# Latent attention in a fused two-block kernel: scores of two head pairs at once in four PSUM banks, the rotated parts of four heads on quarters of the array rows

## The reference

```python
def mla_mixer(xn, w_in, q_norm, w_uq, kv_norm, w_ukv, w_o, cos_r, sin_r):
    c = xn @ w_in                                   # 1024 -> 384 + 256 + 32
    cq  = rms_norm(c[..., :384], q_norm)
    ckv = rms_norm(c[..., 384:640], kv_norm)
    kr  = c[..., 640:]                              # one rotated key of 32, shared by all heads
    qf = (cq @ w_uq).reshape(B, S, 16, 64 + 32)
    q_rope = apply_rope(qf[..., 64:], cos_r, sin_r)
    kv = (ckv @ w_ukv).reshape(B, S, 16, 64 + 64)
    k_rope = broadcast(apply_rope(kr, cos_r, sin_r))
    q = concat([qf[..., :64], q_rope]); k = concat([kv[..., :64], k_rope]); v = kv[..., 64:]
    o = causal_attention(q, k, v, scale=96 ** -0.5) # 16 heads, softmax over keys <= query
    return o.reshape(B, S, 1024) @ w_o
```

## Time and profile before

| | |
|---|---|
| median of 3 runs | 1077.17 us (1076.83 to 1077.51) |
| the profiled execution's own time | 1076.59 us |
| span from its first to its last instruction | 1074.8 us |
| PE busy | 1069.1 us (99%) |
| PE weight loads busy | 935.4 us (87%) |
| DVE busy | 839.1 us (78%) |
| ACT busy | 655.6 us (61%) |
| DMA | 191.67 MB, 178 GB/s on average |

### The profile page before, as it was taken

The page is one execution under the profiler, slowest core; times in us unless marked ns, Lnnn a source line. Parts: engine busy times, 40 slices in busy tenths (PEclk is TensorE's granted clock), DMA queues, the critical chain, the costliest instruction groups (busy, mean ns, idle before and its releaser), DMA issues.

```text
span 1074.8 us, 16290 instructions
## 1 busy us (share of the span) xinstructions
PE 1069.1 (99%) x6536; PEld 935.4 (87%) x6536; DVE 839.1 (78%) x1364; ACT 655.6 (61%) x923; POOL 1.3 (0%) x8
## 2 busy tenths in 40 slices
PE   9999999999999999999999999999999999999998
PEld 7778888888898888888889888888977788888888
DVE  7985799886667689988767999776658768997852
ACT  7666567664467765766456577554456765776540
POOL 0000000000000000000000000000000000000000
PEclk9999999999999999999999999999999999999999
DMA  8543446556426064655552366555555434665540
GB/s 318 202 171 119 151 166 234 194 186 215 164 88 245 2 225 163 232 200 187 213 191 109 127 227 235 186 216 186 179 184 181 144 123 150 234 216 193 205 144 30
DMA packets 32091, 191.67 MB, mean 178 GB/s; under 512 B 4496, under 2 KB 6160, under 8 KB 12176
## 3 DMA queue, kind: packets, MB, share of 16 engines
q1 hardware_dynamic: 32016, 190.63, 49.8%
HBM read 189.56 MB, written 1.05 MB: 177 GB/s over the span
## 4 chain that ended last, share of the span: by engine, by line
PE 97%; DVE 1%; ACT 1%; DMA 0%; SPq 0%; issue 0%; DVEq 0%
PE banks L452 21%; PE SB L452 11%; PE TB L452 11%; PE banks L454 11%; PE TB L454 6%; PE SB L454 6%; PE banks L667 4%; PE banks L674 4%; PE banks L668 4%; PE banks L411 4%; PE banks L413 3%; PE banks L412 3%; PE banks L621 2%; PE TB L596 2%; PE SB L583 1%; PE SB L1000 1%
## 5 line engine op out<-in xcount | busy, mean ns | idle before, releaser
L1658 DVE TENSOR_TENSOR wlo<-raw,whi 128x2048 fp32r<-128x2048 f32 (+2 forms) x180 | 396.1, 2202 | 75.1 <-ACT whi L1134 75.0
L1134 ACT ACTIVATE whi<-raw 128x2048 fp32r<-128x2048 f32 (+2 forms) x180 | 330.5, 1840 | 83.8 <-PE TB L454 25.6
L452 PE MATMUL banks<-xx,whi 128*128 128x512 f32 x752 | 262.0, 390 | 0.0
L454 PE MATMUL banks<-xx,wlo 128*128 128x256 f32 x752 | 212.1, 282 | 0.0
L452 PEld LDWEIGHTS banks<-xx,whi 128*128 128x128 f32 x752 | 141.2, 188 | 29.5
L454 PEld LDWEIGHTS banks<-xx,wlo 128*128 128x128 f32 x752 | 142.1, 189 | 0.0
L452 PE MATMUL TB<-xx,whi 128*128 128x512 f32 x336 | 117.8, 390 | 0.3 <-DVE xx L1663 0.3
L452 PE MATMUL SB<-xx,whi 128*128 128x512 f32 x320 | 111.8, 390 | 0.0
L454 PE MATMUL TB<-xx,wlo 128*128 128x256 f32 x336 | 94.7, 282 | 0.0
L452 PE MATMUL banks<-hx,whi 128*128 128x512 f32 x264 | 91.7, 390 | 0.0
L454 PE MATMUL SB<-xx,wlo 128*128 128x256 f32 x320 | 90.2, 282 | 0.0
(11 more groups left out here) (239 smaller groups left out, 1946.0 us busy)
## 6 DMA issues: line engine op xcount, KB each, us to landing
raw<-in_gate SPq DMA_DIRECT2D x44, 1024.0 KB, 4.8
raw<-in_up SPq DMA_DIRECT2D x44, 1024.0 KB, 4.8
raw<-in_down SPq DMA_DIRECT2D x32, 1024.0 KB, 4.8
raw<-in_down SPq DMA_DIRECT2D x16, 768.0 KB, 4.1
raw<-in_d_kq SPq DMA_DIRECT2D x8, 1024.0 KB, 5.0
raw<-in_a_kq SPq DMA_DIRECT2D x6, 1024.0 KB, 5.3
raw<-in_a_o SPq DMA_DIRECT2D x4, 1024.0 KB, 4.9
raw<-in_b_o SPq DMA_DIRECT2D x4, 1024.0 KB, 5.4
```

Source lines behind the costliest of these rows:

```text
L452: e.matmul(po[:, 0:512], wh[:, k, sl], a[:, kk, :, :].rearrange("p w s -> p (w s)"), start=start, stop=stop, skip_group_check=True)
L454: return e.matmul(po[:, 0:256], wl[:, k, sl], a[:, kk, 0, :], start=False, stop=stop, skip_group_check=True)
L1134: e.activation(whi[n % RING][:, 0:nk * w], raw[n % RAW][:, 0:nk * w], ACT.Copy).then_inc(s_hi, 1)
L1658: e.tensor_tensor(wlo[n % RING][:, 0:nk * w], raw[n % RAW][:, 0:nk * w], whi[n % RING][:, 0:nk * w].bitcast(F32), ALU.subtract).then_inc(s ...
```

## The change

It touches stage B alone.

1. Scores are computed for two pairs (a group, g = 0 to 3) at once, into four banks: `SB` for the even pair and `banks0` for the odd one. `pair_scores(j)` becomes `group_scores(g)`.
2. The rotated part of the four heads of a group is computed on four quarters (32) of the array rows, one head and one bank each. `krt` holds the key once and needs no zeros; ACT copies it in one activation in place of two.
3. The banks are dealt out anew: `values` has one bank (3) in place of two, so `values(j)` waits for `output_lo(j-1)` and not for `output_lo(j-2)`; `queries(2)`, `queries(3)` and `value_block(1, 1)` share bank 2; the projection goes to bank 2 (c = 0) and, once the last scores are out, bank 0 (c = 1).
4. The order of the stage is written anew on PE, ACT and DVE. The number of instructions of each kind stays as it was, except for the one activation.

```diff
-        krt = sb("krt", [128, 2, S], F32, mla)
+        krt = sb("krt", [128, S], F32, mla)
...
+        def score_banks(s, j):
+
+            return two_banks[FLIP[s]] if s == B and j % 2 else SB
+
+        def out_bank(s, c):
+
+            return bk(s, (2, 0)[c]) if s == B else bk(s, c)
...
             if s == B:
-                return bk(s, 2 + j % 2)
+                return bk(s, 3)
...
-                        e.wait_ge(s_ol, n_pair(s, j - 2))
+                    else:
+                        e.wait_ge(s_ol, n_pair(s, j - 1))
...
+                def group_scores(g):
+
+
+                    if g == 0:
                         e.wait_ge(s_krt, 1)
-                    if j % 2 == 0:
-                        e.wait_ge(s_qne, j // 2 + 1)
-                        e.wait_ge(s_kne, j // 2 + 1)
-                    if j % 4 == 0:
-                        e.wait_ge(s_qre, j // 4 + 1)
-                    if j >= 1:
-                        e.wait_ge(s_msk, n_pair(s, j - 1))
...
+                    else:
+                        e.wait_ge(s_msk, n_pair(s, 2 * g - 1))
+                    e.wait_ge(s_qne, g + 1)
+                    e.wait_ge(s_kne, g + 1)
+                    e.wait_ge(s_qre, g // 2 + 1)
+                    blocks = ((0, 128, 128), (128, 256, 256))
+                    for j in (2 * g, 2 * g + 1):
+                        for q0, q1, k1 in blocks:
+                            for a in range(2):
+                                p = slice(64 * a, 64 * a + 64)
+                                e.matmul(score_banks(s, j)[:, a, q0:q0 + k1], qn[p, j, q0:q1], kn[p, j, 0:k1],
+                                         start=(q0 == 0), stop=False, skip_group_check=True)
+                    for q0, q1, k1 in blocks:
+                        for t in range(4):
+                            p = slice(32 * t, 32 * t + 32)
+                            last = e.matmul(score_banks(s, t % 2)[:, t // 2, q0:q0 + k1], qr[p, g, q0:q1], krt[p, 0:k1],
+                                            start=False, stop=True, skip_group_check=True)
+                    last.then_inc(s_sc, 2)
...
-                pair_scores(0)
+                group_scores(0)
+                queries(2)
+                group_scores(1)
+                transposes(s, 0)
                 value_block(1, 1)
-                pair_scores(1)
-                queries(2)
-                pair_scores(2)
+                values(s, 0)
+                transposes(s, 1)
                 queries(3)
-                for j in range(8):
-                    transposes(s, j)
-                    if j < 5:
-                        pair_scores(j + 3)
-                    if j >= 5:
-                        project_01(s, u + 10, [j - 2])
-                    values(s, j)
-                    if 1 < j < 5:
-                        project_01(s, u + 10, [j - 2])
-                project_01(s, u + 10, [6, 7])
+                values(s, 1)
+                transposes(s, 2)
+                group_scores(2)
+                values(s, 2)
+                transposes(s, 3)
+                rows(0, 0, 1)
+                values(s, 3)
+                rows(0, 2)
+                transposes(s, 4)
+                group_scores(3)
+                values(s, 4)
+                transposes(s, 5)
+                rows(0, 3, 4)
+                values(s, 5)
+                rows(1, 0, 1, 2)
+                transposes(s, 6)
+                rows(0, 5)
+                values(s, 6)
+                rows(1, 3)
+                transposes(s, 7)
+                rows(1, 4)
+                rows(0, 6)
+                values(s, 7)
+                rows(1, 5, 6)
+                rows(0, 7)
+                rows(1, 7)
```

(`rows(c, ks)` is the output projection into one of the two banks alone, for the pairs `ks`.) The order on DVE, written out after `normalize(1)`:

```diff
+                pair(3)
+                normalize(s, 2)
+                output_lo(s, 0)
+                normalize(s, 3)
+                output_lo(s, 1)
+                lo(u + 12)
+                pair(4)
+                output_lo(s, 2)
+                pair(5)
+                normalize(s, 4)
+                output_lo(s, 3)
+                normalize(s, 5)
+                pair(6)
...
+                output_lo(s, 7)
+                lo(u + 13)
+                lo(u + 14)
```

More of the change, by code:

```diff
@@ L947, in value_block @@
                     else:
-                        e.wait_ge(s_qne, h + 1)
+                        e.wait_ge(s_qne, 1 + 2 * h)
                     for k in range(2):
-                        last = three(bk(s, 2 + h)[:, :], ox[:, 6 + k, 0, sl], ox[:, 6 + k, 1, sl], wh[:, k, :],
+                        last = three(bk(s, 2 + (h if c == 0 else 0))[:, :], ox[:, 6 + k, 0, sl], ox[:, 6 + k, 1, sl], wh[:, k, :],
                                      wl[:, k, :], k == 0, k == 1)
@@ L970, in queries @@
                         weights_here(n)
[L971 to L975, removed]
+                    e.wait_ge(s_ve, b + 1)
+                    last = channels(n, bk(s, (2, 3, 2, 2)[b]), (b % 2) * 256, 3, 3, b)
                     last.then_inc(s_used if b % 2 else s_qn, 1)
@@ new lines, in group_scores, with rows @@
+                    for q0, q1, k1 in blocks:
[4 more added lines that the diff above has]
+                    last.then_inc(s_sc, 2)
+                def rows(c, *ks):
+                    for k in ks:
+                        if k == 0:
+                            weights_here(u + 10 + c)
+                            e.wait_ge(*((s_qne, 4) if c == 0 else (s_msk, n_pair(s, 7))))
+                        e.wait_ge(s_ol, n_pair(s, k))
+                        last = across(u + 10 + c, out_bank(s, c), k, ox, k, k == 0, k == KD - 1)
+                        if k == KD - 1:
+                            last.then_inc(s_used, 1)
@@ L1480, in key_rope @@
                     e.wait_ge(s_lt, 3)
-                    for m in range(2):
-                        last = e.activation(krt[:, m, :], LT[2], ACT.Copy, scale=evenodd[:, m:m + 1])
-                    last.then_inc(s_krt, 1)
+                    e.activation(krt[:, :], LT[2], ACT.Copy).then_inc(s_krt, 1)
                 def keys(b):
@@ L1497, in value_block @@
                         e.wait_ge(s_vp, c + 1)
-                    e.activation(vv[:, h, c * 512:(c + 1) * 512], bk(s, 2 + h)[:, :],
+                    e.activation(vv[:, h, c * 512:(c + 1) * 512], bk(s, 2 + (h if c == 0 else 0))[:, :],
                                  ACT.Copy).then_inc(s_ve, 1)
@@ L1549, in latent_mixer @@
                 exponentials(s, 1)
-                queries(3)
-                for j in range(8):
-                    weights_turned(s, j)
-                    if j < 6:
-                        exponentials(s, j + 2)
-                    if j in (6, 7):
-                        hi(u + 7 + j)
-                    output_hi(s, j)
+                weights_turned(s, 0)
+                value_block(1, 1)
+                exponentials(s, 2)
+                output_hi(s, 0)
+                weights_turned(s, 1)
+                queries(3)
+                exponentials(s, 3)
+                output_hi(s, 1)
+                weights_turned(s, 2)
+                output_hi(s, 2)
+                weights_turned(s, 3)
+                exponentials(s, 4)
+                output_hi(s, 3)
+                weights_turned(s, 4)
+                exponentials(s, 5)
+                output_hi(s, 4)
+                weights_turned(s, 5)
+                exponentials(s, 6)
+                output_hi(s, 5)
+                exponentials(s, 7)
+                weights_turned(s, 6)
+                output_hi(s, 6)
+                weights_turned(s, 7)
+                hi(u + 13)
+                output_hi(s, 7)
+                hi(u + 14)
                 mixer_end(s, u + 10)
@@ L2157, in latent_mixer @@
                 normalize(s, 1)
-                for j in range(8):
-                    if j < 5:
-                        pair(j + 3)
-                    output_lo(s, j)
-                    if j < 6:
-                        normalize(s, j + 2)
-                    if j >= 5:
-                        lo(u + 7 + j)
+                pair(3)
[11 more added lines that the diff above has]
+                pair(6)
+                output_lo(s, 4)
+                pair(7)
+                normalize(s, 6)
+                output_lo(s, 5)
+                normalize(s, 7)
+                output_lo(s, 6)
+                output_lo(s, 7)
+                lo(u + 13)
+                lo(u + 14)
                 mixer_end(s, u + 10)
```

38 lines of the change are left out of this document (9 added, 29 removed).

## The result

The changed kernel takes 1079.83 us (median of 9 runs, 1079.28 to 1080.3), the kernel before beside it 1077.00 (9 runs, 1076.63 to 1077.51). The ratio is 1.0026, 95% interval [1.0017, 1.0035]: slower, where I had forecast 1077.7 and no change, and 0.4 us above my range.

A forecast was written before the change was run, and what follows sets the result against it. PE was taken to bound the kernel, with 97% of the span. New waits of 3.3 less 2.8 of PE's work saved gave +0.5 us, so a median of 1077.7 us; range 1074.2 to 1079.4.

The forecast's parts named there:

- PE's work: Stage B on PE: rotated parts on quarters save 2.56 us, fewer changes of array shape another 0.2; together 2.8 us less.
- change of shape: On PE, switching the shape in which the array is used costs 0.2 us; 27 such switches before, 26 after.
- a group's rotated part: On PE in stage B, four heads on four quarters start together and cost about 0.84 us per group.
- Six waits: In stage B the new orders make PE stand still six times for DVE or ACT, together 3.3 us.
- waits 4 and 5: `transposes(4)` waits for `normalize(4)`, 1.1 us; `transposes(5)` waits for `normalize(5)`, 0.9 us.
- 2 and 3: `values(1)` waits for `output_lo(0)` and `values(3)` for `output_lo(2)`, 0.4 us each.
- 6: `values(6)` waits for `weights_turned(6)`, 0.3 us.
- Behind the stage: After stage B, DVE reaches the residual 2.2 us later, but `lo(u+17)` still lands in time for F1, 0.3 to spare.
- the rival of a delay carried on: After stage B, DVE's extra lateness makes F1 wait for `lo(u+17)` and so on: above 1079.4 us; chance 0.05.
- quarters one after another: In stage B's scores, products run one at a time, 2.8 us per group: about 1083.5 us; chance 0.06.
- Quarters bring no more than halves: In stage B's scores, four 32-row products run two by two, 1.3 + 0.2 per group: net +1.7, 1078.9 us; chance 0.09.
- The waits stay away: In stage B, DVE and ACT come round sooner, leaving only PE's saving: 1074.4 us; chance 0.16.

The follow-up runs named there:

- experiment 1: Changed kernel with one unused 32-byte tile per partition behind the constants, putting tiles such as `hx` and `ox` back at their old addresses: 1077.59 us, ratio 1.0005.
- experiment 7: Changed kernel with 32 unused bytes behind `con` (old addresses) and stage B's orders on PE, ACT and DVE redrawn: 1074.16 us, ratio 0.9975 against the kernel before.
- experiment 4: Changed kernel with rotated parts on halves again, `evenodd` and the key's second copy back (so old addresses): 1078.36 us, ratio 1.0014 against the kernel before.
- experiment 11: Kernel before with 32 unused bytes ahead of `xx` and 96 behind it: 1086.85 us, ratio 1.0091.

## Why the prediction was wrong, by its own steps

**The step that failed** is the sum's silent one: all terms lie in stage B, and of what was removed elsewhere the prediction says only "the one `krt` activation in place of two is off the path". The removed columns `evenodd` were not costed. They carry no time themselves, but without them every tile behind `con` starts 32 bytes earlier, and that costs 2.1 us (experiment 1: 1079.83 - 1077.59 = 2.24, less 0.17 by which before differed between the two sets). In the profile of the changed kernel it is 0.8 ahead of the stage, 0.13 in it (45.62 against 45.49) and 1.03 behind it. No rival had this mechanism; I had not asked where the tiles lie.

**The sum of the stage was right.** Forecast +0.5, measured +0.56 in the trace of experiment 1 and +0.8 in its time: 1077.6 with the tiles in place, where I had 1077.7.

- *PE's work, -2.8*: -2.9 where almost no wait is left (experiment 7). Its order has one change of shape fewer than the changed kernel's (25 against 26, counted as the prediction counts them), 0.2 by the prediction's price, so about -2.7 for the changed kernel's own order. The price of a group's rotated part was 0.87 for 0.84. The Trainium skill, "TensorE: Matmul & The Clock Gate", section on the measured speedup of packed matmuls, would have given 0.83 and the change of shape, 1.03; it states the 3.07 for 512 columns, where the products here stream 128 and 256. The trace has 0.67 without the change (0.87 - 0.2), an estimated factor of 3.8 (4 x 0.64 / 0.67), so the measurement is nearer to four.
- *Six waits, 3.3*: the traces show five in the list and one of about 0.1, 2.6 to 2.7 in all of PE standing still. To that comes what PE takes to get back in step: in the chain `values` behind a wait takes 0.88, not 0.81. Experiment 1's busy time fell by only 2.1 where its order should save about 2.7, so the restarts cost some 0.6 for six waits, an estimate. Together 3.3, as forecast. Apart: waits 4 and 5 1.7 (forecast 1.1 + 0.9), 2 and 3 0.7 (0.4 + 0.4), 6 0.2 (0.3).
- *Behind the stage*: F1 without a wait for `lo(u+17)`, as forecast; the rival of a delay carried on did not come.
- *The rivals*: quarters one after another fell with the timeline of the changed kernel. "Quarters bring no more than halves" fell with experiments 4 and 7; its price of 1.5 was for quarters that run two by two, with the change of shape, and experiment 4 has true halves without one, 1.34. So its 1078.36 and the rival's 1078.9 are not the same case. "The waits stay away" is what experiment 7 builds: 1074.2 where I had 1074.4.

**What stays open** is the rule behind L. The runs show that moving `hx` and `ox`, or `xx`, lengthens some of the matmuls that stream them, that which ones (256 or 512 columns) differs from place to place, and that neither the remainder by 64 nor by 128 explains all of it. That it is `hx` and `ox` themselves and not a tile behind them is argued from their groups' durations; in experiment 11 the groups that stream `xx` grew, while one that holds `xx` and streams `whi` kept its 395 ns (another, at 407 to 409 ns in the other kernels, read 410). So I take it that the streamed side counts, and the held one does not.

## What to carry to other kernels

A removed or resized tile is an edit to every tile declared behind it: compare the tiles' start bytes before and after, and when work outside the change gets slower without a wait, put the addresses back with a pad before looking for anything else. On a path that one engine holds throughout, a saving is worth what the other engines' queues let through: here about 2.7 us of work saved became +0.8 in time, and with the orders redrawn for it -2.7. Lay the queues end to end with the trace's durations before choosing an order; it gave each wait's place, and the two longest together to 0.3 us.

## What the runs showed of the hardware

- The start of the streamed tiles `hx` and `ox` in the partition, in the kernel before with the same instructions (bytes added up from the declarations): byte 150944 1076.8 us; 150976 1082.1; 151008 1081.1; 151040 1081.3; 151072 1077.9 (there the small tiles were 32 bytes on as well). In the changed kernel 150912 against 150944: +2.1. With `xx` at 115904 in place of 115872: +9.0. In the groups that grew, 512-column matmuls go from 390 to between 391 and 399 ns and most 256-column ones from 279 to between 280 and 285, at the same granted clock; one kind of 256-column group got shorter in some places (282 to 280 ns).
- Four products on quarters of the array rows, into four banks, start within 0.02 us of one another, and a group's set of 16 takes 0.87 us with the change of shape; the same scores on halves take 1.34 without one (experiment 4).
- A matmul group that starts behind a wait takes longer than the same group in step, 0.88 against 0.81 for `values`; by the estimate above, a wait costs about 0.1 us more than the profile shows as standing still.
